# Splitting the low-part subtraction of the projection weights between VectorE and GpSimd

## The chip, the cores and the metric

One core of a Trainium2 chip runs the kernel. The metric is the time of one execution on the device in microseconds. The matrix engine is called PE or TensorE; DVE is VectorE, ACT is ScalarE, POOL is GpSimd and SP is SyncE. A core has SBUF, its working memory of 128 partitions, and PSUM, into which PE writes.

## The reference

A decoder block over one sequence of 256 tokens with 1024 features:

```python
h = rmsnorm(x, norm_mix)
proj = h @ w_in                        # 1024 x 5928, float32
(aq, ak, av, iq, iw, ik, bq, bf, bi, bg, ga, gb) = split(proj)
y_a = dsa_sparse_attention(...)        # index scores, the best 64 keys per query, 8 heads
o_b = hgrn2_chunkwise(...)             # gated linear recurrence, 4 heads
y_b = rmsnorm(o_b) * silu(bg)
merged = sigmoid(ga) * (y_a @ w_up_a) + sigmoid(gb) * (y_b @ w_up_b)
x = x + merged @ w_out
x = x + moe_ffn(rmsnorm(x, norm_ffn))  # the best 4 of 32 experts per token
out = rmsnorm(x, norm_final)
```

All inputs and outputs are float32.

## The kernel before

**Stages.** The projections and the token mixers come first (0 to about 208 us), then the up projections, the merge and the output projection (to about 265 us), the router, and from 282 us a loop over work items of the experts, which takes the rest. In it each item loads six blocks of 2 MB of expert weights.

**Chunks.** The weights up to the output projection come in chunks numbered 0 to 15. A chunk is 128 partitions x 4096 float32 columns, 2 MB. Chunks 1 to 11 are slices of `w_in`, in this order: the attention's query, key and value (1 to 3), the recurrence's query, forget gate, input and gate (4 to 7), and the two merge gates (8 to 11). Chunk 0 is the smaller slice of the indexer. Chunks 12 and 13 are `w_up_a` and `w_up_b`. SP's queue loads chunk n into slot n % 3 of `ring` once PE has used up the chunk that was there (`w_used`).

**High and low parts.** Chunks 1 to 13 are multiplied in a rounded format, in two parts each. `take_high(n)` on ACT (L808) copies the chunk, rounded, into a high slot (slot 3 + n % 3) and raises `high_ready`. `take_low(n)` on DVE (L978) waits for `high_ready`, subtracts the high part from the chunk and writes the rest, rounded, back into the chunk's own slot; it raises `low_ready`. PE multiplies the high part first (L407 and L408, or L420 and L421 for chunks 3 and 6), then waits in `low_part(n)` for the low part, and does L412 or L425. This happens in the first half of a chunk (`project(n, 0)`), the second half needs no further wait.

**Order on each engine.** Each engine has one queue, whose order is written out by hand. The DVE's around the change is:

- `take_low(1)`, the lower bound of the gate (L983 to L986), the indexer's copies (L997 to L1001)
- `take_low(2)`, `take_low(3)`, the index selection of the second token block (`top_keys`: L1008, seven of L1010, L1012, then eight times the maximum and its replacement, L1014 and L1015, then the mask, L1016 and L1017)
- `take_low(4)`, the copy of the keys (L1026) for which PE waits before chunk 4, the selection of the first token block
- `take_low(5)`, `take_low(6)`, the recurrence's query (L1034), `take_low(7)`, the gates (L1039, L1041)
- logits and their maxima (L1048, L1051), the diagonal (L1057, L1059), `take_low(8)`
- eight levels of the recurrence (`next_level`: L1076, L1083, L1084, L1085), for each of which PE does matmuls (L517) and then waits for `level_ready`; between them the scaling of the probabilities (L1094), which PE then transposes (L489), and `take_low(9)` to `take_low(12)`
- the norm of the recurrence's output (L1114, L1117), `take_low(13)`, then L1123 and L1127, which make `y_b` and its low part; PE waits for that before the second up projection (L592)
- the merge (L1137 to L1139), eight times

GpSimd has little to do: small roots for the norms (L1266, L1269), two additions of the index mask to the attention bias (L1283, of 2048 and 1024 columns, each released by `masks_ready` from L1017), and one subtraction like `take_low`'s over 2048 columns (L1287).

Of the kernel before, what the change touches and what calls it, by code (L numbers as in the profile page):

```python
# [17 lines left out]
F32 = mybir.dt.float32  # L18
# [3 lines left out]
ALU = mybir.AluOpType  # L22
# [29 lines left out]
CHUNK = 4096  # L52
N_PRE = len(ORDER) + 4
RAW = 3
LEVELS = 7


def slot_of(chunk):

    return chunk % RAW if chunk < N_PRE - 1 else RING - 1  # L60


def high_slot(chunk):
    return RAW + chunk % RAW


PRE_LOADS = [sum(slot_of(n) == s for n in range(N_PRE)) for s in range(RING)]
USED_BEFORE = [PRE_LOADS[s] if s < RAW else 0 for s in range(RING)]
MOE_SLOT = [0, 3, 1, 4, 2, 5]


def t5_bucket(dist):

    exact = BUCKETS // 2
    if dist < exact:
        return max(dist, 0)
    return min(exact + int(math.log(dist / exact) / math.log(MAX_DIST / exact) * (BUCKETS - exact)),
               BUCKETS - 1)


def shape_constants():
# [12 lines left out]

    levels = np.zeros((P, LEVELS, P // 2), np.int32)
    for l in range(LEVELS):
        size = 1 << l
# [5 lines left out]
    for c in range(PITCH):  # L103
        onehot[t5_bucket(S - 1 - c), c] = 1.0
    return consts, levels.reshape(P, LEVELS * P // 2), onehot


def build(nc, x, w_in, w_up_a, w_up_b, w_out, norm_mix, norm_ffn, norm_final, hgrn_norm, lb_logits,
          rel_bias, w_router, b_router, w_gu, b_gu, w_down, b_down, consts, levels, onehot, out):
    ctx = ExitStack()  # L110
    with ctx:
        def sb(name, words, dt=F32, parts=P):
            return ctx.enter_context(nc.sbuf_tensor(name, [parts, words], dt))

        def sem(name):
            return ctx.enter_context(nc.semaphore(name))
# [3 lines left out]
        with ExitStack() as views:  # L120
            def rounded(name, words):
                return views.enter_context(nc.sbuf_tensor(name, [P, words], F32R))

            slot_r = [rounded(f"slot_r{s}", CHUNK) for s in range(RING)]
# [5 lines left out]
        ring = ctx.enter_context(nc.sbuf_tensor("ring", [P, RING, CHUNK], F32))  # L130
# [15 lines left out]
        cst = sb("cst", 4 * P + S + 4 + NE)  # L146
        lvl = sb("lvl", LEVELS * P // 2, I32)
        tiny = sb("tiny", 576)
# [92 lines left out]
        xn_ready, xT_done, hT_ready = sem("xn_ready"), sem("xT_done"), sem("hT_ready")  # L241
        hT_high_ready, hT_low_ready, x_back = sem("hT_high_ready"), sem("hT_low_ready"), sem("x_back")
        x_high_ready, x_low_ready = sem("x_high_ready"), sem("x_low_ready")
        high_ready, low_ready = sem("high_ready"), sem("low_ready")
        y_a_low_ready, y_b_high_ready, y_b_low_ready = (
            sem("y_a_low_ready"), sem("y_b_high_ready"), sem("y_b_low_ready"))
        blocks_zero = sem("blocks_zero")
# [66 lines left out]
        def _(sp):  # L314
            for r in range(NT):
                sp.dma_start(xr[:, r, :], x[0, r * P:(r + 1) * P, :]).then_inc(x_in[r], 16)
            for n in range(N_PRE):
# [12 lines left out]
                if n == N_PRE - 1:  # L330
                    sp.wait_ge(w_used[slot_of(len(ORDER) - 1)], len(ORDER) // RAW)
                elif n >= RAW:
                    sp.wait_ge(w_used[s], n // RAW)
                if n < len(ORDER):
# [45 lines left out]
        def _(pe):  # L380
# [9 lines left out]
                    last.then_inc(done, 1)  # L390

            def low_part(n):
                pe.wait_ge(low_ready, n)

            def keep_warm(n, bank):

# [3 lines left out]
            def half_T(n, half):  # L400

                (high, low), b = split_parts(n, IN_FORM), 2 * (n % 2) + half
                for c in range(2):
                    dst = psum[:, b, c * S:(c + 1) * S]
                    cols = slice((2 * half + c) * P, (2 * half + c + 1) * P)
                    for j in range(NJ):
                        mm(dst, high[:, j, cols], hT_high[:, j, :], start=(j == 0), stop=False)  # L407
                        mm(dst, high[:, j, cols], hT_low[:, j, :], start=False, stop=False)  # L408
                    if half == 0 and c == 0:
                        low_part(n)  # L410
                    for j in range(NJ):
                        last = mm(dst, low[:, j, cols], hT_high[:, j, :], start=False, stop=(j == NJ - 1))  # L412
                return last

            def half_tok(n, half):

                (high, low), b = split_parts(n, IN_FORM), 2 * (n % 2) + half
                rows = slice(half * P, (half + 1) * P)
                for j in range(NJ):
                    mm(psum[:, b, :], hT_high[:, j, rows], high[:, j, :], start=(j == 0), stop=False)  # L420
                    mm(psum[:, b, :], hT_low[:, j, rows], high[:, j, :], start=False, stop=False)  # L421
                if half == 0:
                    low_part(n)
                for j in range(NJ):
                    last = mm(psum[:, b, :], hT_high[:, j, rows], low[:, j, :], start=False, stop=(j == NJ - 1))  # L425
                return last
# [83 lines left out]
            def level(l):  # L510

                pe.wait_ge(level_ready, l + 1)
                dst = psum[:, 6 + l % 2, :]
                if l < LEVELS:
                    for g in range(BH * NT):
# [61 lines left out]
            for h in range(BH):  # L577
                cols = slice(h * P, (h + 1) * P)
# [29 lines left out]
            pe.wait_ge(y_a_low_ready, 1)  # L608
            pe.wait_ge(high_ready, up_a)
            low_part(up_a)  # L610
            pe.wait_ge(evacuated[0], len(ORDER) // 2)
            pe.wait_ge(evacuated[1], len(ORDER) // 2)
# [17 lines left out]
            for r, half in halves:  # L630
                cols = slice(r * D + half * 512, r * D + (half + 1) * 512)
# [308 lines left out]
        def _(dve):  # L940
            v = nc.vector
# [27 lines left out]
            for r in range(NT):  # L969
                dve.wait_ge(hT_high_ready, r + 1)  # L970
                cols = slice(r * P, (r + 1) * P)
# [3 lines left out]
            def take_low(n):  # L975

                dve.wait_ge(high_ready, n)
                v.tensor_tensor(slot_r[slot_of(n)][:, :], ring[:, slot_of(n), :],  # L978
                                slot_r[high_slot(n)][:, :].bitcast(F32), ALU.subtract).then_inc(low_ready, 1)

            take_low(1)
            dve.wait_ge(lb_exp, 1)
            link(v.tensor_tensor(lbm, lb0, lb1, ALU.add))  # L983
# [34 lines left out]

            take_low(2)
            take_low(3)  # L1020
            top_keys(1, 1, score1, relu1)
            take_low(4)
# [42 lines left out]
            def next_level(l, products):  # L1065

                dve.wait_ge(level_mm, l + 1)
                size = 1 << l
                if l == LEVELS:
                    v.tensor_copy(crossT, psum[:, 6 + l % 2, :].rearrange("p (h t) -> p h t", h=BH)).then_inc(mix_ready, 1)  # L1070
# [50 lines left out]
            for h in range(BH):  # L1121
                cols = slice(h * S, (h + 1) * S)
# [9 lines left out]
            for m in range(NJ):  # L1132
                cols = slice(m * S, (m + 1) * S)
# [117 lines left out]
            for r in range(NT):  # L1251
                dve.wait_ge(final_rs, r + 1)
                for half in range(2):
                    cols = slice(half * 512, (half + 1) * 512)
# [4 lines left out]
        @block.gpsimd  # L1259
        def _(pool):  # L1260
            g = nc.gpsimd
            steps = [0]

            def root(dst, src, width, n, done):

                g.tensor_scalar(src, src, 1.0 / width, EPS, ALU.mult, ALU.add).then_inc(pool_step, 1)  # L1266
                steps[0] += 1
                pool.wait_ge(pool_step, steps[0])
                g.tensor_tensor(dst, src, minus_half.broadcast_to([P, n]), ALU.pow).then_inc(done, 1)  # L1269

            g.memset(row_max[0][:, 0:1], 0.0)
            g.memset(idx_region[:, 512:1024], 0.0).then_inc(cell_zero, 1)
            g.memset(idx_region[:, 1024:1536], 0.0).then_inc(blocks_zero, 1)
            g.memset(qk_region[:, 1024:3072], 0.0).then_inc(blocks_zero, 1)
            pool.wait_ge(consts_in, 16)
            for r in range(NT):
                pool.wait_ge(squares, r + 1)
                root(rs[:, r:r + 1], ss[:, r:r + 1], D, 1, rs_ready)

            pool.wait_ge(bias_in, 32)  # L1280
            for n, (sc, bias, keys) in enumerate(((score1, bias1, S), (score0, bias0, P))):
                pool.wait_ge(masks_ready, n + 1)
                g.tensor_tensor(bias, bias, sc.unsqueeze(1).broadcast_to([P, AH, keys]), ALU.add).then_inc(bias_ready, 1)  # L1283
            pool.wait_ge(o_squares, 1)
            root(o_rs, o_ss, BD, NT * BH, o_rs_ready)
            pool.wait_ge(x_high_ready, 2)
            g.tensor_tensor(x_low, x_sb[:, :], x_high.bitcast(F32), ALU.subtract).then_inc(x_low_ready, 1)  # L1287
            pool.wait_ge(merge_mm, NJ)
            g.memset(y_sb, 0.0).then_inc(y_ready, 1)
            g.memset(combT_sb, 0.0).then_inc(combT_ready, 1)  # L1290

            def mean_root(r, done):

                g.tensor_scalar(ms[:, 2 * r:2 * r + 1], ms[:, 2 * r:2 * r + 1], ms[:, 2 * r + 1:2 * r + 2], EPS,
                                ALU.add, ALU.add).then_inc(pool_step, 1)
                steps[0] += 1
                pool.wait_ge(pool_step, steps[0])
                g.tensor_tensor(rs[:, r:r + 1], ms[:, 2 * r:2 * r + 1], minus_half, ALU.pow).then_inc(done, 1)

            for r in range(NT):  # L1300
                pool.wait_ge(squares, NT + 2 * (r + 1))
                mean_root(r, rs_ready)
            for r in range(NT):
                pool.wait_ge(final_ss, 2 * (r + 1))
                mean_root(r, final_rs)
# [23 lines left out]
```

## Time and profile before

| | |
|---|---|
| median of 3 runs | 1233.81 us (1233.02 to 1234.17) |
| the profiled execution | 1234.17 us |
| its span in the profile | 1231.7 us |
| busy: PE, PE weight load | 1142.2 us (93%), 516.3 us (42%) |
| busy: DVE, ACT, POOL | 310.4 us (25%), 221.9 us (18%), 30.5 us (2%) |
| `take_low` (L978) | 13 instructions, 59.5 us |
| `take_high` (L808) | 13 instructions, 47.0 us |
| moved by DMA | 444.31 MB, 361 GB/s over the span |

The span runs from the first to the last instruction of the profiled execution; the execution's own time has some 2.5 us around it. Times below are microseconds from the span's start. An instruction's duration includes what it waits for after it has started. A bracket at a row's end tells how long the engine sat idle before it and what released it.

### The profile page before, as it was taken

To read this page: it belongs to the slowest core of one execution; us is meant where nothing else is said; L and a number is where in the kernel's file an instruction comes from. 1 tells how busy PE (TensorE), PEld (TensorE's weight loads), DVE (VectorE), ACT (ScalarE), POOL (GpSimd) and SP (SyncE) were. 2 spreads that over 40 slices of the span, in tenths; PEclk is the share of its full clock that TensorE was granted. 3 is DMA by queue.
4 is the path that set the end of the run, shared out by engine and by line. 5 is a ranking of instruction groups with operands and counts; after the bars stand their busy time and mean duration, and the time that the engine had idled before them with its cause. 6 is when DMAs were issued, how large, how long until landed. Compare 5 with 4: busy or idle time off the path is not lost.

```text
span 1231.7 us, 14935 instructions
## 1 busy us (share of the span) xinstructions
PE 1142.2 (93%) x5904; PEld 516.3 (42%) x5904; DVE 310.4 (25%) x561; ACT 221.9 (18%) x296; POOL 30.5 (2%) x27
## 2 busy tenths in 40 slices
PE   8799999999999999999999999999999989999997
PEld 5688999763333333333333323333333223333332
DVE  4298745423111111112111111111111111111111
ACT  3334533011111111111111111111111111111111
POOL 1022000100000000000000000000000000000000
PEclk8899999989999999999999999999999999999999
DMA  7743345656999999999999999999999999999995
GB/s 253 217 144 137 137 149 185 274 230 273 410 420 422 421 422 422 421 421 422 422 422 426 421 424 420 424 422 422 424 419 424 421 422 424 420 424 421 422 424 202
DMA packets 72873, 444.31 MB, mean 361 GB/s; under 512 B 4344, under 2 KB 8728, under 8 KB 56472
## 3 DMA queue, kind: packets, MB, share of 16 engines
q1 hardware_dynamic: 68400, 437.82, 86.7%
q10 hardware_dynamic: 4456, 6.23, 2.1%
q8 instruction: 14, 0.23, 0.1%
q14 instruction: 3, 0.02, 0.0%
HBM read 441.41 MB, written 2.62 MB: 361 GB/s over the span
## 4 chain that ended last, share of the span: by engine, by line
PE 58%; DMA 25%; DVE 8%; SPq 6%; ACT 2%; issue 2%; POOL 0%; ACTq 0%; DVEq 0%; POOLq 0%
PE psum L731 24%; DMA ring<-in_w_gu 21%; PE psum L764 12%; SPq L359 6%; PE psum L693 3%; DMA rel_rows<-hg 3%; PE psum L665 2%; PE psum L412 2%; PE psum L407 2%; PE psum L408 2%; PE psum L744 2%; DVE slot_r L978 1%; DVE hg L1242 1%; DVE hg L1245 1%; DVE hg L1240 1%
## 5 line engine op out<-in xcount | busy, mean ns | idle before, releaser
L731 PE MATMUL psum<-ring,hg 128*64 128x512 f32 x2048 | 462.0, 595 | 23.4 <-DMA ring<-in_w_gu 23.1
L731 PEld LDWEIGHTS psum<-ring,hg 128*64 128x64 f32 x2048 | 142.1, 137 | 330.8 <-issue 250.5
L764 PE MATMUL psum<-ring,hg 128*64 128x512 f32 x1024 | 233.8, 598 | 8.0 <-ACT hg L926 8.0
L764 PEld LDWEIGHTS psum<-ring,hg 128*64 128x64 f32 x1024 | 67.7, 136 | 130.7 <-issue 115.1
L924 ACT ACTIVATE hg<-hg 128x512 f32<-128x512 f32 x32 | 20.1, 630 | 523.6 <-DVE hg L1239 523.6
L1236 DVE COPY qk_region<-psum 128x512 f32<-128x512 f32 x32 | 22.1, 692 | 265.9 <-PE psum L693 265.9
L407 PE MATMUL psum<-hT_r,slot_r 128*128 128x256 f32 x288 | 74.7, 295 | 9.6 <-ACT slot_r L808 8.2
L1239 DVE TENSOR_SCALAR hg<-psum 128x512 f32<-128x512 f32 x32 | 22.1, 692 | 235.9 <-PE psum L731 235.9
L1230 DVE TENSOR_SCALAR idx_region<-cst,tiny 128x128 f32 x64 | 19.3, 344 | 239.5 <-PE psum L764 238.0
L408 PE MATMUL psum<-x_r,slot_r 128*128 128x256 f32 x288 | 73.4, 291 | 0.0
L978 DVE TENSOR_TENSOR slot_r<-ring,slot_r 128x4096 fp32r<-128x4096 f32 x13 | 59.5, 4588 | 28.7 <-ACT slot_r L808 28.6
L707 PE MATMUL psum<-hg 64*128 64x512 f32 x264 | 65.6, 615 | 0.3 <-ACT hg L932 0.3
L693 PE MATMUL psum<-work,idx_region 128*64 128x512 f32 x264 | 62.3, 592 | 0.0
L407 PEld LDWEIGHTS psum<-hT_r,slot_r 128*128 128x128 f32 x288 | 57.6, 200 | 11.0 <-ACT slot_r L808 9.0
L808 ACT ACTIVATE slot_r<-ring 128x4096 fp32r<-128x4096 f32 x13 | 47.0, 3621 | 65.1 <-DMA ring<-in_w_in 27.8
L408 PEld LDWEIGHTS psum<-x_r,slot_r 128*128 128x128 f32 x288 | 57.6, 200 | 0.0
L752 PE MATMUL psum<-cst,hg 128*128 128x128 f32 x128 | 21.0, 287 | 29.7 <-DVE hg L1245 29.7
L412 PE MATMUL psum<-hT_r,slot_r 128*128 128x256 f32 x288 | 41.9, 290 | 2.9 <-DVE slot_r L978 2.9
L924 ACT ACT_TABLE_LOAD x32 | 41.1, 1283 | 0.9 <-issue 0.3
L707 PEld LDWEIGHTS psum<-hg 64*128 64x128 f32 x264 | 22.7, 186 | 42.1 <-issue 41.5
L412 PEld LDWEIGHTS psum<-hT_r,slot_r 128*128 128x128 f32 x288 | 38.4, 198 | 3.4 <-DVE slot_r L978 3.4
L932 ACT ACTIVATE hg<-psum 128x512 f32<-128x512 f32 x32 | 19.1, 597 | 102.7 <-PE psum L764 102.7
(237 smaller groups left out, 782.8 us busy)
## 6 DMA issues: line engine op xcount, KB each, us to landing
ring<-in_w_gu SPq DMA_DIRECT2D x128, 2048.0 KB, 25.4
ring<-in_w_down SPq DMA_DIRECT2D x64, 2048.0 KB, 23.2
ring<-in_w_in SPq DMA_DIRECT2D x11, 2048.0 KB, 8.2
ring<-in_w_out SPq DMA_DIRECT2D x2, 2048.0 KB, 14.1
ring<-in_w_up_a SPq DMA_DIRECT2D x1, 2048.0 KB, 10.6
ring<-in_w_up_b SPq DMA_DIRECT2D x1, 2048.0 KB, 7.8
rel_rows<-hg ACTq DMA_DIRECT2D x1, 1536.0 KB
ring<-in_w_in SPq DMA_DIRECT2D x1, 1184.0 KB, 9.1
```

The costliest lines, as they stand in the source:

```text
L359: sp.dma_start(slot_gu(c), src).then_inc(w_loaded[s], 16)
L407: mm(dst, high[:, j, cols], hT_high[:, j, :], start=(j == 0), stop=False)
L408: mm(dst, high[:, j, cols], hT_low[:, j, :], start=False, stop=False)
L412: last = mm(dst, low[:, j, cols], hT_high[:, j, :], start=False, stop=(j == NJ - 1))
L665: last = mm(psum[:, 4 + 2 * r + half, :], mergedT[:, m, r * P:(r + 1) * P], slot4(s)[:, m % 4, half * 512:(half + 1) * 512], start=False, ...
L693: last = mm(psum[half * 64:half * 64 + 64, 3, :], pick[:, r, :], h2[:, r, 4 * half:4 * half + 4, :].rearrange("p j q -> p (j q)"), start=( ...
L707: return mm(psum[:, 4 + 2 * r + half, :], combT_sb[rows, r * P:(r + 1) * P], y_sb[rows, :], start=False, stop=True, skip_group_check=True)
L731: last = mm(psum[half * 64:half * 64 + 64, b, :], xgT_sb[:, a:a + SLOTS], slot_gu(c)[:, jj, c0:c0 + 512], start=(j == 0), stop=(j == NJ - ...
L764: last = mm(psum[half * 64:half * 64 + 64, 2, :], actT_sb[:, a:a + SLOTS], slot4(s)[:, k, half * 512:(half + 1) * 512], start=(m == 0), st ...
L808: f(slot_r[high_slot(n)][:, :], ring[:, slot_of(n), :], ACT.Copy).then_inc(high_ready, 1)
L924: f(sig_sb, gate_sb, ACT.Sigmoid, scale=ALPHA).then_inc(sigm_ready, 1)
L978: v.tensor_tensor(slot_r[slot_of(n)][:, :], ring[:, slot_of(n), :], slot_r[high_slot(n)][:, :].bitcast(F32), ALU.subtract).then_inc(low_re ...
```

## The change

The 4096 columns of a chunk's low part are divided. GpSimd subtracts columns 0 to 2559, DVE columns 2560 to 4095. Both wait for `high_ready`; each raises a semaphore of its own, and PE waits for both. DVE's calls of `take_low` stay where they are. GpSimd's 13 calls are put between its other work: 1 to 4 before the first bias addition, 5 behind it, 6 behind the second, 7 to 12 next, 13 after the root for the recurrence's norm.

```diff
+POOL_COLS = 2560
...
-        high_ready, low_ready = sem("high_ready"), sem("low_ready")
+        high_ready, low_pool, low_dve = sem("high_ready"), sem("low_pool"), sem("low_dve")
...
             def low_part(n):
-                pe.wait_ge(low_ready, n)
+                pe.wait_ge(low_pool, n)
+                pe.wait_ge(low_dve, n)
...
             def take_low(n):

                 dve.wait_ge(high_ready, n)
-                v.tensor_tensor(slot_r[slot_of(n)][:, :], ring[:, slot_of(n), :],
-                                slot_r[high_slot(n)][:, :].bitcast(F32), ALU.subtract).then_inc(low_ready, 1)
+                cols = slice(POOL_COLS, CHUNK)
+                v.tensor_tensor(slot_r[slot_of(n)][:, cols], ring[:, slot_of(n), cols],
+                                slot_r[high_slot(n)][:, cols].bitcast(F32), ALU.subtract).then_inc(low_dve, 1)
...
+            def take_low(n):
+
+                pool.wait_ge(high_ready, n)
+                cols = slice(0, POOL_COLS)
+                g.tensor_tensor(slot_r[slot_of(n)][:, cols], ring[:, slot_of(n), cols],
+                                slot_r[high_slot(n)][:, cols].bitcast(F32), ALU.subtract).then_inc(low_pool, 1)
+
+            for n in range(1, 5):
+                take_low(n)
             pool.wait_ge(bias_in, 32)
             for n, (sc, bias, keys) in enumerate(((score1, bias1, S), (score0, bias0, P))):
                 pool.wait_ge(masks_ready, n + 1)
                 g.tensor_tensor(bias, bias, sc.unsqueeze(1).broadcast_to([P, AH, keys]), ALU.add).then_inc(bias_ready, 1)
+                take_low(5 + n)
+            for n in range(7, 11):
+                take_low(n)
+            take_low(11)
+            take_low(12)
             pool.wait_ge(o_squares, 1)
             root(o_rs, o_ss, BD, NT * BH, o_rs_ready)
+            take_low(13)
```

## Rows read from the trace of the kernel before

**Rows 1.** The page's chain that ended last, shares of the span by line.

```profile
PE psum L731 24%; DMA ring<-in_w_gu 21%; PE psum L764 12%; SPq L359 6%; PE psum L693 3%; DMA rel_rows<-hg 3%; PE psum L665 2%; PE psum L412 2%; PE psum L407 2%; PE psum L408 2%; PE psum L744 2%; DVE slot_r L978 1%; DVE hg L1242 1%; DVE hg L1245 1%; DVE hg L1240 1%
```

**Rows 2.** Windows: bounds, length, busy us by engine, granted clock, DMA share.

```profile
core 0: us, PE busy (x) PEld busy (x) DVE busy (x) ACT busy (x) POOL busy (x), PEclk, DMA share, GB/s
55.00:99.00 44.00, 39.94 (x260) 36.26 (x260) 41.90 (x76) 21.59 (x11) 12.55 (x2) 0.96 0.45 152
99.00:208.00 109.00, 108.61 (x844) 103.93 (x845) 71.81 (x60) 46.33 (x55) 4.42 (x3) 0.98 0.42 144
99.40:103.00 3.60, 3.60 (x18) 3.60 (x19) 3.60 (x1) 0.00 (x0) 2.17 (x1) 0.56 0.95 355
```

**Rows 3.** Timeline of PE where it waits: start, us, line, idle before.

```profile
59.73 1.22 PE L412 MATMUL psum<-hT_r,slot_r 128*128 128x256 f32 x8 [0.74 <-DVE slot_r L978]
...
83.62 0.36 PE L407 MATMUL psum<-hT_r,slot_r 128*128 128x256 f32 x1 [1.40 <-DVE qk_region L1026]
...
99.39 1.76 PE L412 MATMUL psum<-hT_r,slot_r 128*128 128x256 f32 x8 [2.11 <-DVE slot_r L978]
```

**Rows 4.** Waits, 0 to 330 us: total, times, longest.

```profile
DVE qk_region L1076 <- PE psum L517: 18.0, 5, 8.6
...
PE psum L592 <- issue: 1.0, 1, 1.0
```

**Rows 5.** All 13 instructions of L978: duration in ns, minimum, median, maximum.

```profile
L978 DVE TENSOR_TENSOR slot_r<-ring,slot_r x13: 4415/4421/6591, 23.9 to 207.4; 128x4096 fp32r<-128x4096 f32 x13
```

**Rows 6.** Timeline of DVE and PE around the first levels of the recurrence.

```profile
136.22 1.34 DVE L1076 COPY_PREDICATED qk_region<-lvl,psum 128x512 f32<-128x512 int32 x1 [0.74 <-PE psum L517]
...
139.56 2.29 DVE L1094 TENSOR_TENSOR work<-work,tiny 128x2048 f32<-128x2048 f32 x1
...
141.76 1.90 PE L517 MATMUL psum<-hg 128*128 128x64 f32 x16
...
143.50 1.04 PE L489 MATMUL psum<-cst,work 128*128 128x128 f32 x8
```

**Rows 7.** Timeline of POOL, its three large instructions.

```profile
76.92 8.63 POOL L1283 TENSOR_TENSOR bias_region<-bias_region,score 128x2048 f32<-128x2048 f32 x1 [67.21 <-DVE score L1017]
95.08 6.48 POOL L1283 TENSOR_TENSOR bias_region<-bias_region,score 128x1024 f32<-128x1024 f32 x1 [9.54 <-DVE score L1017]
...
219.62 4.62 POOL L1287 TENSOR_TENSOR x_r<-x_sb,work_r 128x2048 fp32r<-128x2048 f32 x1 [13.37 <-ACT work_r L897]
```

**Rows 8.** Timeline of DVE at the same times and in the selections.

```profile
64.31 3.61 DVE L1010 SCALAR_TENSOR_TENSOR score<-work,tiny,score 128x256 f32<-128x256 f32 x7
...
76.69 4.42 DVE L978 TENSOR_TENSOR slot_r<-ring,slot_r 128x4096 fp32r<-128x4096 f32 x1
...
81.02 2.45 DVE L1026 COPY qk_region<-psum 64x1024 f32<-64x1024 f32 x2
...
83.50 2.12 DVE L1008 TENSOR_SCALAR score<-work,tiny 128x128 f32<-128x128 f32 x1
85.67 2.68 DVE L1010 SCALAR_TENSOR_TENSOR score<-work,tiny,score 128x128 f32<-128x128 f32 x7
...
94.92 10.93 DVE L978 TENSOR_TENSOR slot_r<-ring,slot_r 128x4096 fp32r<-128x4096 f32 x2
...
219.80 4.71 DVE L1139 TENSOR_TENSOR hT_region<-work 128x256 f32<-128x256 f32 x1
```

**Rows 9.** Timeline of ACT: high parts of chunks 2 and 3, 8, and 9.

```profile
51.53 7.12 ACT L808 ACTIVATE slot_r<-ring 128x4096 fp32r<-128x4096 f32 x2 [27.69 <-issue]
...
127.24 3.61 ACT L808 ACTIVATE slot_r<-ring 128x4096 fp32r<-128x4096 f32 x1
...
134.88 3.63 ACT L808 ACTIVATE slot_r<-ring 128x4096 fp32r<-128x4096 f32 x1 [3.12 <-DMA ring<-in_w_in]
```

**Rows 10.** Timeline of DVE before the second up projection.

```profile
207.43 4.42 DVE L978 TENSOR_TENSOR slot_r<-ring,slot_r 128x4096 fp32r<-128x4096 f32 x1
...
211.76 1.65 DVE L1123 SCALAR_TENSOR_TENSOR hg<-psum,tiny,silu_g 128x256 f32<-128x256 f32 x4
...
214.54 1.23 DVE L1127 TENSOR_TENSOR hg_r<-hg,hg_r 128x1024 fp32r<-128x1024 f32 x1 [1.12 <-ACT hg_r L894]
```

## The prediction

> **What bounds the kernel now.** I read the chain that ended last first: by line its largest parts are the expert loop's matmuls and the expert weights' loads [rows 1]. That loop begins at 282 us, holds none of the changed instructions, and starts when the stages before it have ended. So the change can only move the point where the loop starts, and each microsecond there is one of the whole. The windows come next. Between 55 and 99 us VectorE is busy 41.9 of 44 us and PE 39.9; from 99 to 208 us PE is busy 108.6 of 109 us [rows 2]. The first stretch has two owners that wait for each other; in the second PE sets the pace, and VectorE is late only if its delay outgrows its slack. PE waits for VectorE at four places: 0.7 us for the low part of chunk 2, 1.4 us for the copy of the keys (L1026), 2.1 us for the low part of chunk 5 [rows 3], and 1.0 us before the second up projection [rows 4] (the view puts it down to issue; it ends 0.1 us after L1127, for which PE's queue waits there).
>
> **Prices.** VectorE's subtraction over 4096 columns takes 4.42 us, once 6.59 [rows 5]; one over 2048 columns of two SBUF operands takes 2.29 [rows 6]. The slope is 2.13 us per 2048 columns, so 1536 columns cost 2.29 - 0.53 = 1.76 us, of which 1.7 hold the next instruction up. GpSimd did 2048 such columns in 4.62 us alone [rows 7], so 2560 cost 5.77 at most.
>
> **The rows that decide.** GpSimd's bias add (2048 columns) started at 76.92 and took 8.63 us [rows 7]. VectorE's subtraction had started at 76.69 and ended at 81.11 [rows 8]; 85.55 - 81.11 = 4.44 us is GpSimd's own work, so 2560 columns cost 5.55 by this row. I take 5.6. It did nothing while VectorE subtracted. The reverse stands beside it: VectorE's L1008, 128 columns long, began at 83.50 and ended at 85.62, with the bias add [rows 8]. At 94.92 two subtractions of VectorE follow each other while the second bias add waits from 95.08: 10.93 us against 2 x 4.42, and the add ends at 101.56, 2.2 us after the first subtraction [rows 7, 8]. So they exclude each other (below I call it a lock), and whoever waits is served when the other's instruction ends, even if that engine has another one queued. At 219.80 an addition of 256 columns takes 4.71 us beside GpSimd's 4.62 [rows 7, 8]. The copies from PSUM (L1026, 2.45 us for two) ran inside the bias add at full speed [rows 8]: one that reads PSUM is left alone. L1008 has one SBUF tensor operand only and waited, so simple scalar operations on SBUF data count as hit.
>
> The Trainium skill (SBUF — State Buffer, "Who interferes with whom") calls the shared pair of ports an exclusive lock, held for the whole instruction, where the second to issue blocks fully. By it every VectorE operation of two SBUF inputs behind a GpSimd subtraction waits up to 5.6 us; a sharing of bandwidth would let the new parts overlap and give the rival on the other side below. The page has no order for three waiting instructions; the row at 94.92 has.
>
> **What the change does to one chunk.** Before, one instruction of 4.42 us. Now 1.7 on VectorE and 5.6 on GpSimd exclude each other though one semaphore releases both: the low part is whole 7.3 us after the high part, 2.9 later than before. VectorE saves 4.42 - 1.7 = 2.7 us per chunk, 13 times, and for 13 x 5.6 = 73 us it may not start an operation of two SBUF operands or a fast scalar one (L1008, L1010, L1039, L1083 to L1085, L1094, its own subtraction). Whether that costs depends on what VectorE has to do then, so I walk it.
>
> **Walk to 111 us.** Chunk 1: VectorE 23.9 to 25.6, GpSimd to 31.2; what is queued behind on VectorE (L983 onward) starts about 1.4 us late, and PE wants its results only at 43.3. Nothing. Chunk 2: high part ready at 55.15 [rows 9]. VectorE to 56.9, GpSimd to 62.5. PE went on at 59.73 [rows 3]; now 62.5, +2.8. This stall is covered by the next ones. Chunk 3's high part is ready at 58.7; VectorE waits until 62.5, subtracts to 64.2, GpSimd takes its part until 69.8. VectorE's index selection (L1008, then seven L1010 from 64.31 [rows 8]) meets that lock: L1008 at 69.8. GpSimd has chunk 4 queued (high part ready at 66.0) and comes in between L1008 and the first L1010: 70.1 to 75.7. The L1010s start at 75.7, +11.4. GpSimd then waits for the mask. The selection ends at 88.1; chunk 4's part on VectorE saves 2.7, so L1026 ends at 92.2 and PE starts chunk 4 there, not at 83.62 [rows 3]: +8.7. GpSimd's bias add runs from 89.8 to 94.2, L1008 of the second selection waits for it as it did before, GpSimd's part of chunk 5 follows at 94.5 to 100.1, and the L1010s that began at 85.67 [rows 8] begin at 100.1: +14.4. The selection ends at 109.3, VectorE's part of chunk 5 at 111.0. PE, which went on with it at 99.39 [rows 3], now does at 111.1. **First term: +11.7 us.** PE's own delays (chunk 2's stall, the slower clock behind it) lie inside this, because PE reaches that wait at 107.7.
>
> **Walk from 111 to 170 us.** The second bias add ends at 113.2, VectorE's part of chunk 6 at 114.9, GpSimd's at 120.5, chunk 7's at 127.8. L1039 waits for that last lock, so the logits (L1048) are done at 132.2, where PE, itself 11.7 late, asks for them at 131.4. **Second term: +0.8 us.** Chunk 8's high part, made from 127.24 before [rows 9], now ends at 145.8, chunk 9's at 151.1 (134.88 + 3.6 before, and PE's 12.5). VectorE's part of chunk 8 ends at 147.6; GpSimd holds the lock to 153.2. The first level of the recurrence (L1076 onward, at 136.22 before [rows 6]) comes at 148.7; L1083 waits until 153.2. Then GpSimd's part of chunk 9 steps in behind L1083, 153.9 to 159.5; L1084 and L1085 end at 160.9, the scaling of the probabilities (2.29 us) at 163.4. PE did level 1 at 141.76 and the transposes of the probabilities at 143.50 [rows 6]: it would reach level 1 at 154.3, waits until 160.9, and starts the transposes at 163.4, 19.9 late. **Third term: +7.4 us.** If chunk 9's high part comes 2 us later, GpSimd's 5.6 fall on the next operations of the same line of work, at about the same price.
>
> **After 170 us.** Chunks 10 to 12 on GpSimd meet VectorE in its levels, where it had idled 18.0 us in five waits for PE [rows 4]. In my walk they push L1083 by about 2 us twice, inside that slack: 0; at most, with the whole 5.6 against the mean idle time of 3.6, 2.0 each. Chunk 13: its high part is ready at 206.5; GpSimd has it until 212.2, VectorE, there at 207.43 [rows 10], waits and ends at 213.9, not 211.8. Behind it stand L1123 and L1127 [rows 10], and PE already waits for them [rows 4]. **Fourth term: +2.1 us.**
>
> **The clock.** After its wait of 2.1 us PE was granted 0.56 of full speed for 3.6 us [rows 2], which costs about 1.6 us; after its 0.7 us wait, nothing. The 6.6 us stall at level 1 costs up to 1.6, half of it hidden until 163.4: 0.8. The stall before the second up projection grows from 1.0 to 3.1 us: 1.6, at least 0. **Fifth term: +2.4.**
>
> **Sum.** 11.7 + 0.8 + 7.4 + 2.1 + 2.4 = 24.4 us. The profiled execution took 1234.17 us (span 1231.7); with the sum 1258.6. The median of the runs is 0.36 below it, so 1258.
>
> **Rivals.** (a) Milder: two or three of the GpSimd parts that I set against the short operations of VectorE (those of chunks 4, 5 and 9, 5.6 us each) fall where nothing is held up, in its maxima for instance, whose behaviour no row shows. Two less give 1247, three 1241. For it: a difference of 0.3 us decides who is first. Chance 0.14. One less gives 1252 and is within the forecast's own range. (b) VectorE's dependent short operations keep the port until the selection is over: it starts 5.9 late and wins back 2 x 2.7, first term +0.5; with the second and fourth, the third and the clock at next to nothing, 3.4 to 4 more than before, 1238. No row shows a queue of short operations against a waiting GpSimd, but the alternation at 94.92 speaks against. 0.05. (c) Harsher: levels after 170 us too, and more slow clock: 1265 to 1270. 0.11. (d) **Faster:** the two engines run side by side. Then the low part is ready 5.8 us after the high one, which costs PE 1.3 at chunk 2, but the waits of 1.4 and 2.1 us with 1.6 of slow clock behind the latter and the 1.0 before the up projection go: 4.8 less, 1229. It decides if the price of overlap per chunk stays under VectorE's saving, 2.7 us; the rows show a whole wait, 4.2 of 4.4. 0.05. (e) No measurable change, if PE's slack took all: 0.03.
>
> **How the numbers follow.** The forecast, 1250 to 1264, has 0.62. From 1240 to 1265 lie it, (a) and half of (c): 0.81. A change under 0.2% (2.5 us) can't be told from none here. Slower by more than that: 0.92; within it 0.03; faster 0.05.
>
> **What would show it.** In the new profile GpSimd's 13 parts should show 5.6 us where VectorE leaves it alone and some 7.3 where it comes second; VectorE's parts 1.7 alone and up to 7.3 behind GpSimd; single L1008, L1010, L1083 or L1084 operations of over 5 us; PE waiting for VectorE at chunks 2 and 5 and at level 1; the expert loop starting near 306 us and taking as long as before. Wrong would be: overlapping parts at their own lengths; GpSimd's parts stretched instead of VectorE's (VectorE served first each time); or PE's waits absent.

## The result, and the profile after

| | median | runs | against before |
|---|---|---|---|
| before | 1233.77 us | 1233.02 to 1234.17 | |
| changed | 1251.95 us | 1251.01 to 1255.9 | 1.0154 (95%: 1.0132 to 1.0176) |

The changed kernel is slower by 18.2 us. The profiled execution took 1252.55 us with a span of 1250.3, which is 18.6 more than before; the ledger below adds up to that. The line numbers of the new kernel are 2 to 18 higher: L981 and L1287 are the two parts of the low part, L1011 and L1013 the selection (L1008, L1010), L1086 to L1088 a level (L1083 to L1085), L414 the low matmuls (L412), L594 the up projections (L592).

From the top of the changed kernel's page:

```profile
span 1250.3 us, 14959 instructions
PE 1144.7 (92%) x5904; PEld 517.0 (41%) x5904; DVE 327.0 (26%) x561; ACT 221.6 (18%) x296; POOL 108.6 (9%) x40
```

VectorE was to be relieved, and is busy for 327.0 us, not 310.4. The groups of instructions of the changed kernel give the reason (total and mean ns of one, then the idle time before):

```profile
L1287 POOL TENSOR_TENSOR slot_r<-ring,slot_r 128x2560 fp32r<-128x2560 f32 x13 | 83.4, 6429 | 98.7 <-ACT slot_r L810 98.7
...
L981 DVE TENSOR_TENSOR slot_r<-ring,slot_r 128x1536 fp32r<-128x1536 f32 x13 | 46.2, 3563 | 30.8 <-ACT slot_r L810 30.7
```

VectorE's 1536 columns take 3.56 us on average where 1.76 would do (13 x 1.76 = 22.9): half of the 46.2 us is waiting. With GpSimd's 83.4 us the 13 subtractions now hold two engines for 129.6 us, where [rows 5] held one for 59.5.

The timelines of GpSimd and VectorE in the changed kernel, from chunk 2 on:

```profile
54.88 20.00 POOL L1287 TENSOR_TENSOR slot_r<-ring,slot_r 128x2560 fp32r<-128x2560 f32 x3 [23.88 <-ACT slot_r L810]
87.67 5.90 POOL L1295 TENSOR_TENSOR bias_region<-bias_region,score 128x2048 f32<-128x2048 f32 x1 [12.79 <-DVE score L1020]
93.53 5.73 POOL L1287 TENSOR_TENSOR slot_r<-ring,slot_r 128x2560 fp32r<-128x2560 f32 x1
...
143.97 13.31 POOL L1287 TENSOR_TENSOR slot_r<-ring,slot_r 128x2560 fp32r<-128x2560 f32 x2 [17.34 <-ACT slot_r L810]
```

```profile
54.91 14.42 DVE L981 TENSOR_TENSOR slot_r<-ring,slot_r 128x1536 fp32r<-128x1536 f32 x2 [20.85 <-ACT slot_r L810]
69.25 5.77 DVE L1011 TENSOR_SCALAR score<-work,tiny 128x256 f32<-128x256 f32 x1
75.06 3.61 DVE L1013 SCALAR_TENSOR_TENSOR score<-work,tiny,score 128x256 f32<-128x256 f32 x7
...
91.59 2.06 DVE L1011 TENSOR_SCALAR score<-work,tiny 128x128 f32<-128x128 f32 x1
93.69 8.04 DVE L1013 SCALAR_TENSOR_TENSOR score<-work,tiny,score 128x128 f32<-128x128 f32 x7
...
122.38 5.36 DVE L1042 TENSOR_SCALAR hg<-hg,tiny 128x256 f32<-128x256 f32 x4 [1.26 <-ACT hg L851]
...
148.72 3.10 DVE L1086 TENSOR_TENSOR hg<-hg 128x512 f32<-128x512 f32 x1
151.73 6.10 DVE L1087 TENSOR_TENSOR hg<-hg 128x512 f32<-128x512 f32 x1
...
227.00 6.44 DVE L981 TENSOR_TENSOR slot_r<-ring,slot_r 128x1536 fp32r<-128x1536 f32 x1
```

Read them as pairs. Chunks 2 to 4 on GpSimd last from 54.88 to 74.88. L1011, 256 columns, began at 69.25 and took 5.77 us, to 75.02; alone it took 0.35. The seven L1013 start at 75.06, where they had started at 64.31 [rows 8], and no part of GpSimd came between L1011 and them. In the second selection one did: L1011 waited until the bias addition had ended at 93.57, and then the seven took 8.04 us, not 2.68, beside GpSimd's part of chunk 5 (93.53 to 99.26). L1042 took 5.36 for what had been 1.38 us of work, beside chunk 7's part. L1086 and L1087, about 0.7 us each alone, took 3.10 and 6.10 beside chunks 8 and 9. VectorE's part of chunk 13 took 6.44 us, 1.76 of them its own.

Where PE waits in the changed kernel:

```profile
62.30 2.05 PE L414 MATMUL psum<-hT_r,slot_r 128*128 128x256 f32 x8 [3.68 <-DVE slot_r L981]
...
91.71 0.55 PE L409 MATMUL psum<-hT_r,slot_r 128*128 128x256 f32 x1 [5.61 <-DVE qk_region L1029]
...
110.19 2.04 PE L414 MATMUL psum<-hT_r,slot_r 128*128 128x256 f32 x8 [2.94 <-DVE slot_r L981]
...
130.73 1.56 PE L482 MATMUL psum<-qk_region 128*128 128x256 f32 x6 [0.52 <-DVE work L1051]
...
158.49 3.68 PE L519 MATMUL psum<-hg 128*128 128x64 f32 x16 [5.22 <-DVE hg L1088]
...
237.46 0.36 PE L594 MATMUL psum<-hg_r,slot_r 128*128 128x256 f32 x1 [3.03 <-issue]
```

The first three are the waits of [rows 3], grown from 0.74, 1.40 and 2.11 us; the last is the 1.0 us of [rows 4], grown to 3.0. Those before L482 and before level 1 (L519) are new. In the latter row the level's 16 matmuls take 3.68 us, not 1.90: the clock is down.

**The ledger.** How late PE is at each of its marks against the trace before:

| mark | before | changed | late |
|---|---|---|---|
| low part of chunk 5 | 99.39 | 110.19 | 10.8 |
| second logits | 119.50 | 130.73 | 11.2 |
| level 1 | 141.76 | 158.49 | 16.7 |
| transposes of the probabilities | 143.50 | 161.96 | 18.5 |
| level 3 | 158.49 | 178.07 | 19.6 |
| second up projection | 215.86 | 237.46 | 21.6 |
| residual matmuls (L632) | 233.29 | 254.80 | 21.5 |
| expert loop (L731) | 282.10 | 300.19 | 18.1 |
| span | 1231.7 | 1250.3 | 18.6 |

The delay grows to 21.5 us at the end of the changed part, and 3.4 come back in the router stretch, which holds nothing of the change. Two windows of each kernel, the whole stretch and six microseconds in it (bounds, length, busy us of PE, PE's weight load, VectorE, ACT, GpSimd, granted clock, DMA share, GB/s); before:

```profile
233.30:282.10 48.80, 46.77 (x172) 28.44 (x171) 13.43 (x46) 7.09 (x17) 2.52 (x6) 0.90 0.62 254
268.00:274.00 6.00, 6.00 (x30) 6.00 (x29) 2.71 (x13) 1.88 (x2) 0.00 (x0) 0.50 0.73 300
```

changed:

```profile
254.80:300.20 45.40, 42.69 (x174) 24.04 (x172) 13.45 (x46) 7.10 (x17) 2.52 (x6) 1.00 0.66 272
289.50:295.50 6.00, 5.50 (x47) 5.12 (x45) 4.01 (x19) 2.55 (x6) 0.00 (x0) 1.00 0.73 295
```

In the first trace PE was granted 0.50 (the 1.2 GHz level) while the router's small matmuls ran, in the second 1.00. The same work took 48.8 and 45.4 us.

### The profile page after: what moved, and what is told of

The parts are those of the page before. It is cut to its first block, busy times and chain, and to the rows that moved or that the text cites. A ratio compares the mean times of both kernels' runs of the same rounds, so it can differ in the third digit from the quotient of the medians.

```text
span 1250.3 us, 14959 instructions
## 1 busy us (share of the span) xinstructions
PE 1144.7 (92%) x5904; PEld 517.0 (41%) x5904; DVE 327.0 (26%) x561; ACT 221.6 (18%) x296; POOL 108.6 (9%) x40
## 4 chain that ended last, share of the span: by engine, by line
PE 54%; DMA 24%; DVE 11%; SPq 6%; ACT 2%; issue 2%; POOL 0%; ACTq 0%; DVEq 0%
PE psum L733 24%; DMA ring<-in_w_gu 21%; PE psum L766 12%; SPq L360 6%; PE psum L695 3%; DMA rel_rows<-hg 3%; PE psum L667 2%; DVE slot_r L981 2%; PE psum L746 2%; PE psum L414 2%; PE psum L409 2%; PE psum L410 1%; DVE hg L1245 1%; DVE hg L1248 1%; DVE hg L1243 1%
## 5 line engine op out<-in xcount | busy, mean ns | idle before, releaser
L1287 POOL TENSOR_TENSOR slot_r<-ring,slot_r 128x2560 fp32r<-128x2560 f32 x13 | 83.4, 6429 | 98.7 <-ACT slot_r L810 98.7
L409 PE MATMUL psum<-hT_r,slot_r 128*128 128x256 f32 x288 | 76.4, 300 | 13.7 <-ACT slot_r L810 8.1
L409 PEld LDWEIGHTS psum<-hT_r,slot_r 128*128 128x128 f32 x288 | 58.9, 204 | 15.1 <-ACT slot_r L810 9.0
L981 DVE TENSOR_TENSOR slot_r<-ring,slot_r 128x1536 fp32r<-128x1536 f32 x13 | 46.2, 3563 | 30.8 <-ACT slot_r L810 30.7
L414 PE MATMUL psum<-hT_r,slot_r 128*128 128x256 f32 x288 | 43.4, 296 | 6.6 <-DVE slot_r L981 6.6
L414 PEld LDWEIGHTS psum<-hT_r,slot_r 128*128 128x128 f32 x288 | 39.9, 205 | 7.0 <-issue 7.0
## 6 DMA issues: line engine op xcount, KB each, us to landing
ring<-in_w_up_a SPq DMA_DIRECT2D x1, 2048.0 KB, 10.8
```

The costliest lines, as they stand in the source:

```text
L981: v.tensor_tensor(slot_r[slot_of(n)][:, cols], ring[:, slot_of(n), cols], slot_r[high_slot(n)][:, cols].bitcast(F32), ALU.subtract).then_i ...
L1287: g.tensor_tensor(slot_r[slot_of(n)][:, cols], ring[:, slot_of(n), cols], slot_r[high_slot(n)][:, cols].bitcast(F32), ALU.subtract).then_i ...
```

## The experiments

Theory: VectorE and GpSimd exclude each other, and the dependent short operations of VectorE pay for it. Rival: GpSimd is only slow, the engines run side by side, and the low part comes late because it has the larger share.

**Parts of the change.** Three kernels divide only some chunks; in the others VectorE keeps all 4096 columns. The edit, with another list in each:

```diff
+SPLIT = (2, 3, 4, 5)
...
-                pe.wait_ge(low_pool, n)
+                if n in SPLIT:
+                    pe.wait_ge(low_pool, SPLIT.index(n) + 1)
...
-                cols = slice(POOL_COLS, CHUNK)
+                cols = slice(POOL_COLS if n in SPLIT else 0, CHUNK)
...
+                if n not in SPLIT:
+                    return
                 pool.wait_ge(high_ready, n)
```

> Only chunks 2 to 5 are divided; the other nine low parts stay whole on VectorE. Theory of exclusion: the first term alone. GpSimd's parts of chunks 2, 3 and 4 fall in front of the first selection, that of chunk 5 in front of the second, so the low part of chunk 5 comes some 10.8 us late as in the changed kernel, and the time is 1243 to 1247 us. Rival (GpSimd is only slow, the engines run side by side): the low parts come 1.2 us later at chunk 2 and VectorE is free earlier, 1229 to 1235 us.

> Only chunks 8 and 9 are divided. Theory of exclusion: GpSimd's two parts, 5.6 us each, stand in front of the first level of the recurrence and of the scaling of the probabilities; PE waits 4 to 6 us before level 1 and then runs on a slower clock for some us: 5.5 to 8 us more than before, 1239 to 1242 us. Rival (side by side): no PE wait there, 1233 to 1234 us.

> Only chunks 10 to 13 are divided. Theory of exclusion: 10, 11 and 12 fall inside VectorE's slack and cost nothing, 13 delays the second up projection by 2.0 us: 1235.8 us. Rival (side by side): chunk 13's part on VectorE ends earlier and the 1.0 us wait of PE goes, 1232.8 us.

The comparisons below are each with the kernel before on the same chip (1231.8 and 1232.07 us there, 1233.77 in the first comparison). The times in the expectations start from 1233.8, so it is the excess over before that is compared. Measured, before 1231.8 us: 1243.84 us (1.0088, 1.0061 to 1.0114) for chunks 2 to 5, 1239.5 us (1.0054, 1.0037 to 1.0071) for 8 and 9, 1235.34 us (1.0026, 1.0011 to 1.0041) for 10 to 13. The first wait of PE that each adds, one row of each kernel in that order:

```profile
109.97 1.41 PE L416 MATMUL psum<-hT_r,slot_r 128*128 128x256 f32 x5 [3.34 <-DVE slot_r L983]
```

```profile
144.20 2.83 PE L521 MATMUL psum<-hg 128*128 128x64 f32 x16 [4.17 <-DVE hg L1090]
```

```profile
217.40 0.55 PE L596 MATMUL psum<-hg_r,slot_r 128*128 128x256 f32 x1 [3.04 <-issue]
```

Chunks 2 to 5 make the low part of chunk 5 10.6 us late and add no later wait. Chunks 8 and 9 add 4.2 us before level 1; from level 0 to level 2 PE takes 22.0 us there, 15.9 before, so 6.1 are lost, slow clock included. Chunks 10 to 12 add no wait at all, and 13 makes the wait of 1.0 us one of 3.0. The rival had an excess of 1.2 us at most for any of the three; it falls three times. The three excesses over before add up to 0.88 + 0.54 + 0.26 = 1.68%, the whole change costs 1.54%; the intervals allow both to be the same, so the terms are nearly independent. Chunks 1, 6 and 7 are in none of the three. The third kernel cost 3.5 us instead of 2.0. In its trace PE ran on the slow clock after the stall (a window of the same kernel):

```profile
217.40:221.40 4.00, 4.00 (x19) 4.00 (x20) 0.93 (x3) 1.91 (x1) 1.68 (x1) 0.50 1.02 410
```

From the stall to the residual matmuls PE took 20.0 us there and 17.4 in the kernel before, so 2.6 are slow clock. That execution took 1237.86 us, the second longest of the ten; that the same happened in most of the others, and makes the median's 1.5 us, isn't shown.

**A balanced split.**

```diff
-POOL_COLS = 2560
+POOL_COLS = 1312
```

> All 13 chunks divided, but GpSimd has only 1312 of 4096 columns: 2.9 us for it and 3.0 for VectorE, the balanced split if the engines ran side by side. Rival (side by side): every low part is ready 3.1 us after its high part, not 4.4, and the waits of 0.7, 1.4 and 2.1 us shrink or go: 1228 to 1231 us. Theory of exclusion: a low part takes 5.9 us, the short operations wait 2.9 us each time instead of 5.6: the low part of chunk 5 some 6 us late, in all 7 to 11 us more than before, 1241 to 1245 us.

Measured: 1239.62 us (1.0065, 1.0045 to 1.0086). That is 7.8 us over before on this chip (1231.8), within the 7 to 11 of the theory (the time itself lies under its 1241 to 1245); the rival forecast 3 to 6 us less than before. The timelines of GpSimd and VectorE in this kernel:

```profile
53.82 3.00 POOL L1287 TENSOR_TENSOR slot_r<-ring,slot_r 128x1312 fp32r<-128x1312 f32 x1 [23.90 <-ACT slot_r L810]
57.33 5.30 POOL L1287 TENSOR_TENSOR slot_r<-ring,slot_r 128x1312 fp32r<-128x1312 f32 x1 [0.51 <-ACT slot_r L810]
```

```profile
53.85 11.70 DVE L981 TENSOR_TENSOR slot_r<-ring,slot_r 128x2784 fp32r<-128x2784 f32 x2 [20.88 <-ACT slot_r L810]
65.47 3.11 DVE L1011 TENSOR_SCALAR score<-work,tiny 128x256 f32<-128x256 f32 x1
```

Here, as in the changed kernel, GpSimd happened to be first by 0.03 us; it worked for 3.0 us undisturbed; VectorE's two parts, 3.05 us each, took 11.70. The smaller share shortens VectorE's waits (L1011: 3.11 us, not 5.77) and doesn't remove them. PE went on with the low part of chunk 5 at 103.62, 4.2 us later than before, or 5.6 if both are counted from PE's first matmul of chunk 2 (53.80 here, 55.20 before); some 6 were expected.

**The exclusion by itself.** Two kernels leave the low parts whole on VectorE, as before, and give GpSimd work that nobody waits for until chunk 8: at every high part of chunks 1 to 8 it subtracts two SBUF operands, or only writes. Both outputs of GpSimd go to a region that is overwritten later.

```diff
+            def work_beside(n):
+                pool.wait_ge(high_ready, n)
...
+                g.tensor_tensor(sig_b[:, :], sig_a[:, :], sig_a[:, :], ALU.subtract).then_inc(extra, 1)
```

In the other kernel the last line is this one, three times:

```diff
+                    g.memset(sig_b[:, :], 0.0).then_inc(extra, 1)
```

> The kernel before, whole low parts on VectorE, and nobody waits for GpSimd's new work until chunk 8: at each high part of chunks 1 to 8 GpSimd subtracts two SBUF operands of 2048 columns (4.5 us) into a region that nothing needs yet. Its output is the reference's. Theory of exclusion: the delay comes from the lock alone, so the kernel is slower without any part of the low part moved: by my walk the low part of chunk 5 comes some 18 us late, in all 15 to 25 us more. Rival (the low part is late because GpSimd is slow and PE waits for it): 1233 to 1235 us.

> As the kernel that subtracts beside, but GpSimd only writes: three memsets of 2048 columns (some 5.5 us together) at each high part of chunks 1 to 8. Theory of exclusion by reads: VectorE's instructions keep their lengths, 1233 to 1235 us. Rival (any long GpSimd instruction holds VectorE up, or the waits and semaphores of the new queue cost): as slow as the kernel that subtracts beside.

Measured, before 1232.07 us on this chip: 1250.51 us (1.0141, 1.0119 to 1.0164) with the subtractions, 1236.27 us (1.003, 1.0016 to 1.0044) with the memsets. A loss as large as the change's appears with every low part still on VectorE: a low part that GpSimd does late isn't needed for it. The two losses are made up differently, though: here the residual matmuls come 17.4 us late, in the changed kernel 21.5. My walk for this kernel was too long, though: the low part of chunk 5 came at 113.74, 14.4 us late and not 18, because this subtraction, of a region from itself, took 3.61 us in the second selection, not 4.5, and four of them stand in front of that low part.

With the subtractions, GpSimd and VectorE:

```profile
56.21 19.08 POOL L1286 TENSOR_TENSOR sig_b<-sig_a 128x2048 f32<-128x2048 f32 x3 [24.39 <-ACT slot_r L808]
```

```profile
56.23 15.60 DVE L980 TENSOR_TENSOR slot_r<-ring,slot_r 128x4096 fp32r<-128x4096 f32 x2 [21.37 <-ACT slot_r L808]
```

With the memsets, GpSimd and VectorE:

```profile
55.11 16.87 POOL L1287 MEMSET sig_b<- 128x2048 f32 x9 [25.94 <-ACT slot_r L808]
...
85.85 5.53 POOL L1287 MEMSET sig_b<- 128x2048 f32 x3
```

```profile
55.15 8.76 DVE L980 TENSOR_TENSOR slot_r<-ring,slot_r 128x4096 fp32r<-128x4096 f32 x2 [20.77 <-ACT slot_r L808]
...
64.61 3.61 DVE L1012 SCALAR_TENSOR_TENSOR score<-work,tiny,score 128x256 f32<-128x256 f32 x7
...
83.82 3.92 DVE L1010 TENSOR_SCALAR score<-work,tiny 128x128 f32<-128x128 f32 x1
```

Beside memsets VectorE's two subtractions take 8.76 us, twice 4.38, and the seven L1012 take 3.61 us, both as without a neighbour [rows 5, 8]. Only scalar operations pay: the L1010 above took 3.92 us, not 2.12, to 87.74, which is the end of the first memset of the row at 85.85; L1010 of the first selection 0.74 us, not 0.35; the four L1041 (L1039 before) 2.02 us, not 1.38. So GpSimd's reads hold up instructions of two SBUF operands, and its writes hold up the scalar one. The long L1010 shows one thing more: it had waited through the bias addition (77.23 to 85.90) and then waited through the memset that GpSimd had queued behind it. With 0.4 us in the first selection that is 2.2 us on the path, and the low part of chunk 5 comes at 101.50, 2.1 late. It makes my expectation of no cost for the memsets wrong by that much. The rest of the 4.2 us (interval 2.0 to 5.4) isn't explained: the profiled execution, 1233.3 us, was the shortest of the ten.

The Trainium skill (SBUF — State Buffer, "Who interferes with whom") names these two cases, two SBUF inputs against a GpSimd instruction that reads, and the 2-port modes of copies and scalar operations against any. These two runs agree, with 8.76 against 15.60 us for the one and 3.92 us for the other.

**An order that makes VectorE less late.** The kernel before, with two low parts moved on VectorE and nothing else:

```diff
-            take_low(4)
             chunk_done(2)
...
             last.then_inc(evacuated[0], 1)
+            take_low(4)
+            take_low(5)
             top_keys(2, 0, score0, relu0)
-            take_low(5)
```

> The kernel before with another order on VectorE only: the copy of the keys before the low part of chunk 4, and the low part of chunk 5 before the second selection. If PE's waits of 1.4 us at chunk 4 and of 2.1 us at chunk 5 (with 1.6 us of slow clock behind it) are what VectorE costs there, the time falls by 3.5 to 5 us, to 1229 or 1230. If another wait takes their place, it stays at 1233 to 1234.

Measured: 1227.47 us, before 1232.07: 0.9958 (0.9942 to 0.9974). That is a fall of 4.6 us, of 3.5 to 5 expected. The waits of 1.40 and 2.11 us are gone; PE has one of 0.17 us left there, for the low part of chunk 4. It is that short because PE came late, on a clock of 0.50 after its 0.75 us wait at chunk 2. The next kernel, with the same order and 1.00 there, waits 1.74 us at this place:

```profile
85.97 1.77 PE L416 MATMUL psum<-hT_r,slot_r 128*128 128x256 f32 x8 [1.74 <-DVE slot_r L983]
```

So another wait takes the place of the first in part.

**The change where it costs nothing.** The same order, with chunk 13 alone divided, 2048 columns each, on top of the changed kernel:

```diff
-POOL_COLS = 2560
+POOL_COLS = 2048
+SPLIT = (13,)
...
-            take_low(13)
             dve.wait_ge(yb_mm, 1)
...
             last.then_inc(yb_ready, 1)
+            take_low(13)
```

> The same order, and chunk 13 alone divided, 2048 columns for each engine, VectorE's part put behind L1123, whose operands come from PSUM and one from SBUF: GpSimd's part runs while VectorE has nothing with two SBUF operands to do. By the exclusion theory the 1.0 us wait before the second up projection goes as well: 1228 or 1229, up to 1 us less than with the new order alone. If GpSimd work always costs, it is slower than the new order alone.

Measured: 1227.28 us, 0.9966 (0.9951 to 0.9982), beside 0.9958 for the order alone. GpSimd and VectorE in it:

```profile
204.97 4.60 POOL L1291 TENSOR_TENSOR slot_r<-ring,slot_r 128x2048 fp32r<-128x2048 f32 x1 [0.30 <-ACT slot_r L812]
```

```profile
207.11 1.66 DVE L1127 SCALAR_TENSOR_TENSOR hg<-psum,tiny,silu_g 128x256 f32<-128x256 f32 x4 [1.19 <-PE psum L608]
208.69 3.03 DVE L983 TENSOR_TENSOR slot_r<-ring,slot_r 128x2048 fp32r<-128x2048 f32 x1
```

L1127, with one operand in PSUM and one in SBUF, ran at full speed beside GpSimd. PE's wait before the second up projection is gone from this trace. The 1 us is not resolved in the times: the two kernels' intervals overlap for the most part. Both beat both given kernels; I would keep the order alone.

**The same two kernels once more,** for the clock.

> The kernel before, unchanged, for a second trace. In the first one the stretch from the residual matmuls (L632) to the expert loop (L731) took 48.8 us and PE's clock was granted at 0.50 in it; in the changed kernel's 45.4 us at 1.00. If that difference belongs to the change, this trace shows 48.8 us again; if it comes and goes by itself, it may show 45 to 46.

> The changed kernel, unchanged, for a second trace. If the router stretch's clock belongs to the change, it takes 45.4 us again; if not, it may take up to 49. By the exclusion theory the residual matmuls start 20 to 23 us later than in the kernel before either way.

The kernel before took 1231.58 us. Its router stretch, in the window of the same bounds in work:

```profile
233.50:279.80 46.30, 43.97 (x174) 25.35 (x172) 13.43 (x46) 7.10 (x17) 2.52 (x6) 0.96 0.66 269
```

46.3 us, where the first trace of the same code shows 48.8. The changed kernel took 1253.74 us, 45.4 of them in this stretch again, but its stall of 3.0 us before the second up projection was now followed by a granted clock of 0.61 for 4 us, and its residual matmuls started at 256.86, 2.1 later than in its first trace, and 23.3 later than in the second trace of the kernel before, a little more than the 20 to 23 expected. Of the 2.1 us, 0.9 were lost between levels 1 and 3 and 1.4 after the stall. In the twelve traces of this study the router stretch takes 45.4 to 49.1 us. It varies with the code unchanged, 48.8 and 46.2 us in the kernel before; but the three traces with 45.4 are those of the kernels with all 13 chunks divided, and no other is under 46.2, so a part of the change in it isn't excluded.

## Why the prediction was right, step by step

Direction and cause were right, and the time, 1252, lies in the range and 6 us under the forecast of 1258. That it is the very time that rival (a) gives for one hit less is chance: no hit was missing, and 3.4 of the 6 us come from the router stretch, where the forecast had nothing. For the same reason the expert loop starts at 300.19 and not near 306.

- **The price per chunk.** GpSimd's part was to cost 5.6 us; undisturbed it takes 5.67 to 5.71. VectorE's was to cost 1.76; alone it takes 1.75 or 1.76. Shown.
- **The first term,** 11.7 us at chunk 5: measured 10.8. The number came out better than the order. The walk had VectorE first at chunk 2, chunk 4's part on GpSimd behind L1008 and the L1010s behind that; in the trace GpSimd was first by 0.03 us, and chunk 4's part ran before L1011 (the old L1008). The same three parts of GpSimd and two of VectorE stand before the selection either way, so the sum is the same, which is luck in the order and not in the exclusion. In the second selection the order was as walked, with chunk 5's part between L1011 and the L1013s. Of the missing 0.9 us, 0.3 are an earlier start of this execution (ACT's part of chunk 2 at 51.19, not at 51.53 as in [rows 9]); the rest was not followed up. The kernel with chunks 2 to 5 alone shows it apart: 10.6.
- **The second,** 0.8 at the logits: 0.4.
- **The third,** 7.4 up to the transposes: PE is 16.7 late at level 1 and 18.5 at the transposes (161.96 against 143.50), so 7.3 since the logits. Chunk 9's part did step in, behind L1086. But 0.9 of the 7.3 belong to the clock: the scaling of the probabilities (L1097) ended at 161.00, and PE, at 0.50 since level 1, took until 161.96 to come to the transposes. The exclusion alone made 6.4, an estimate from these rows. The kernel with chunks 8 and 9 alone shows the term too, 6.1 with slow clock in it.
- **Chunks 10 to 12** cost nothing, as said: 2.70 and 2.45 us L1086 operations, no PE wait. The fourth term, 2.1 for chunk 13: 2.0.
- **The fifth term failed.** I set 2.4 us for slow clock in this part, 0.8 after level 1 and 1.6 after the up projection's stall, and nothing outside it. After level 1 it came to 2.0, the 0.9 above and 1.1 behind the transposes; the 3 us stall before the up projection was followed by full clock. So the sum of the term was near by luck, with both of its parts wrong. And in the router stretch the profiled run before, which I had taken as the base, carried 3.4 us of slow clock that the changed one's trace hadn't. In the sum, with the 0.9 left in the third term: 10.8 + 0.4 + 7.3 + 1.1 + 2.0 = 21.6 where I had 24.4; less 3.4; 0.4 to 0.5 more in the expert loop: 18.6.
- **The rivals.** That the engines run side by side is refuted by the balanced split and by the subtraction beside. The milder case was not needed: the parts of chunks 4, 5, 8 and 9 that I had set against short operations all hit them.
- **A step that doesn't hold in general.** That whoever waits is served when the other's instruction ends was right in the rows above wherever GpSimd's next instruction was a subtraction or an addition. Beside memsets it was not: L1010 waited through two instructions of GpSimd in a row.

What stays open is why the router's clock falls in some executions and stays up in others of the same code. No run here was made to tell, nor whether the divided chunks have a part in it.

## What to carry to other kernels

Work that is moved to GpSimd to relieve VectorE must be set against what VectorE does at that moment. In this kernel 2560 columns on GpSimd cost VectorE's next two-operand or scalar SBUF instruction up to 5.6 us, so a chain of short instructions that PE waits for (a selection, a level of a recurrence) is a bad neighbour, and a stretch of operations with an operand in PSUM was a harmless one (L1026, L1127). Before splitting a late instruction, see whether another order makes it early: moving two low parts ahead of a selection gained 0.42% where the split lost 1.54%.

## What the runs showed of the hardware that was not expected

- GpSimd's writes alone held up VectorE's scalar operation on SBUF data (3.92 us instead of 2.12 for L1010 beside memsets) and left two-operand subtractions alone (4.38 us each).
- Where GpSimd's next queued instruction is a subtraction or addition of SBUF operands, it doesn't keep the turn, and neither does VectorE's. In the changed kernel and in the one with 1312 columns the turns alternate, also when VectorE's instruction is a short one: L1086 comes between the parts of chunks 8 and 9. A scalar operation behind a memset is the exception: L1010 waited through the bias addition and the memset queued behind it.
- The clock that PE is granted after like stalls differs between executions: 1.00 after 3.03 us of waiting in one trace of the changed kernel, 0.61 after 3.05 us in the other, 0.50 after 3.04 us in a third kernel. From there to the residual matmuls PE took 17.3, 18.7 and 20.0 us, so 1.4 and 2.6 us hang on it there, and up to 3.7 in the router stretch (45.4 to 49.1 us), so differences under 4 us between two single traces need the ledger, not the span.
